# How many projection pieces stand in each of a turn's seventeen slots, in a hybrid decoder step on one NeuronCore

## The reference, cut to what matters

```python
n = rms_norm(x, g_mix)
q, k, v, xr, gr, gates = jnp.split(n @ w_in, SPLITS, axis=-1)
attn = attend(q, k, v, ...)                  # 16 heads, stick breaking
xc, rnn_buf_new = causal_dwconv(xr, rnn_buf, w_rnn_conv, b_rnn_conv)
hseq, h_last = rg_lru(xc, rnn_h0, w_rgate, b_rgate, w_igate, b_igate, rglru_lambda)
rnn = hseq * jax.nn.gelu(gr)
gate_a, gate_b = jnp.split(jax.nn.sigmoid(gates), 2, axis=-1)
x = x + (gate_a * attn + gate_b * rnn) @ w_out
...
x = x + (jax.nn.gelu(ua) * ub) @ w_down
```

## Time and profile before

| | us |
|---|---|
| median of 3 runs | 2058.79 (2057.93 to 2062.34) |
| the profiled execution | 2064.17 |
| its span on the core | 2062.5 |
| PE busy in the span | 1899.3 |
| DVE busy | 1211.0 |
| ACT busy | 929.6 |
| time per turn, scores(0) to scores(0), turns 0 to 6 | 101.4, 111.7, 109.5, 112.1, 108.5, 112.3, 108.0 |

### The profile page before, as it was taken

The page is one execution under the profiler, slowest core; times in us unless marked ns, Lnnn a source line. Parts: engine busy times, 40 slices in busy tenths (PEclk is TensorE's granted clock), DMA queues, the critical chain, the costliest instruction groups (busy, mean ns, idle before and its releaser), DMA issues. The chain is left out here.

```text
span 2062.5 us, 38464 instructions
## 1 busy us (share of the span) xinstructions
PE 1899.3 (92%) x14580; PEld 1732.3 (84%) x14580; DVE 1211.0 (59%) x1999; ACT 929.6 (45%) x1506; POOL 199.2 (10%) x98
## 2 busy tenths in 40 slices
PE   6998999989998999898996978999999999999985
PEld 5897878878787878786873768999999999999984
DVE  6101667767685858576776344755665566556655
ACT  5121677776767686768764222222222122212213
POOL 0121000000000000000000003221122112211210
PEclk9999999999999999999997988999999999999998
DMA  3334213131314232332223211211111111101104
GB/s 133 109 87 112 75 47 101 42 105 44 97 44 107 56 85 66 80 83 71 74 58 95 93 62 50 62 51 31 51 51 51 31 51 51 51 31 51 51 10 181
DMA packets 198685, 143.47 MB, mean 70 GB/s; under 512 B 58289, under 2 KB 187890, under 8 KB 198528
## 3 DMA queue, kind: packets, MB, share of 16 engines
q1 hardware_dynamic: 198554, 141.73, 23.9%
HBM read 124.31 MB, written 17.61 MB: 69 GB/s over the span
## 5 line engine op out<-in xcount | busy, mean ns | idle before, releaser
L87 PE MATMUL d_p_up<-n_hi,d_w_hi 128*128 128x346 f32 x1056 | 341.9, 324 | 14.7 <-POOL d_w_lo L1762 7.9
L87 PE MATMUL d_p_up<-n_hi,d_w_lo 128*128 128x346 f32 x1056 | 341.3, 323 | 0.0
L87 PE MATMUL d_p_up<-n_lo,d_w_hi 128*128 128x346 f32 x1056 | 341.0, 323 | 0.0
L1910 DVE TENSOR_TENSOR mix<-mix,d_p_down 128x346 f32<-128x346 f32 x264 | 136.1, 515 | 267.8 <-PE d_p_down L1959 267.8
L87 PE MATMUL b_p_proj<-n_hi,b_w_hi 128*128 128x350 f32 x768 | 264.4, 344 | 15.9 <-DVE b_w_lo L1117 9.4
L1762 POOL TENSOR_TENSOR d_w_lo<-w_raw,d_w_hi 128x1024 fp32r<-128x1024 f32 x45 | 109.1, 2426 | 1483.0 <-ACT d_w_hi L1793 1483.0
L87 PE MATMUL b_p_proj<-n_lo,b_w_hi 128*128 128x350 f32 x768 | 251.4, 327 | 0.0
L87 PE MATMUL b_p_proj<-n_hi,b_w_lo 128*128 128x350 f32 x768 | 251.3, 327 | 0.0
L1807 ACT ACTIVATE d_up<-d_p_up 128x346 f32<-128x346 f32 x132 | 60.1, 457 | 399.6 <-PE d_p_up L87 399.6
L87 PEld LDWEIGHTS d_p_up<-n_hi,d_w_hi 128*128 128x128 f32 x1056 | 200.4, 190 | 16.0 <-POOL d_w_lo L1762 8.3
L87 PEld LDWEIGHTS d_p_up<-n_lo,d_w_hi 128*128 128x128 f32 x1056 | 200.8, 190 | 0.0
(11 more groups left out here) (262 smaller groups left out, 3849.4 us busy)
## 6 DMA issues: line engine op xcount, KB each, us to landing
w_raw<-in_w_in SPq DMA_DIRECT2D x45, 512.0 KB, 4.2
w_raw<-in_w_up SPq DMA_DIRECT2D x45, 512.0 KB, 3.7
b_page<-in_cache_k SPq DMA_DIRECT2D x128, 128.0 KB, 2.1
b_page<-in_cache_v SPq DMA_DIRECT2D x128, 128.0 KB, 2.1
w_raw<-in_w_down SPq DMA_DIRECT2D x22, 512.0 KB, 3.4
b_q_in<-q_scr SPq DMA_DIRECT2D x272, 32.0 KB, 2.2
mix<-in_x_prompt SPq DMA_DIRECT2D x8, 512.0 KB, 7.9
w_raw<-in_w_out SPq DMA_DIRECT2D x8, 512.0 KB, 3.5
```

The costliest lines, as they stand in the source:

```text
L87: last = pe.matmul(out, w[:, k, :], x[:, k, col:col + width], start=(k == 0 and w is w_hi and x is x_hi), stop=(k == KT - 1 and w is w_lo))
L1910: dve.tensor_tensor(to, to, p_down[:, n % 4, 0:FW], ALU.add).then_inc(down_out, 1)
```

## The change

The number of pieces in each slot is changed. The sum stays 96, and the order of the pieces among themselves stays.

```diff
     for s in range(SLOTS):
-        count = 6 if s < 8 or s % 3 == 0 else 5
+        count = 11 if s == 0 else 6 if s < 6 else 5
         here, at = pieces[at:at + count], at + count
```

## The result

| | before | changed |
|---|---|---|
| median | 2060.57 us (4 runs) | 2114.52 us (4 runs, 2112.11 to 2115.93) |
| ratio to before | | 1.0252 (95% interval 1.0235 to 1.0268) |
| profiled span | 2062.5 us | 2114.2 us |

The change costs 52 us (1.0252 x 2060.57 - 2060.57). The forecast was 29 us, and the range ended at 2103 us. The direction and the places were right, a size was not.

The account below looks back on a forecast made before the run. PE was taken as the bound, busy 92% of the span. Turns 1 to 7 at 3.3 us each (23.2 us) plus 5.8 us in turn 0 made 29 us on 2058.8: 2088 us, range 2073 to 2103 us.

Parts of the forecast that it names:

- Part 1: Slot 0: five more pieces cost nothing in turns 1 to 7, and 2.5 us once in turn 0.
- rival E: Turn starts: cover of the fill fails, scores(0) late for ACT; up to 17.5 us more, 2105 us; 7% together with rival C.
- Part 2: Slots 6, 7, 9, 12, 15: one piece less gains 2.0 us a turn, slot 9's not gained; turn 0 gains 2.5 us.
- Parts 3 and 4: New waits: slot 10 for gr1's copy, 3.54 us a turn; slot 13 for gb0's copy, 1.28 us a turn.
- 18.1 us would have spoken against it: Sign against the forecast: slot 10's value products to slot 13's first projection staying 18.1 us, not 21 or more.
- Part 5: Clock: lower level behind slot 10's wait costs 1.5 us a turn (bounds 0 and 4.1); turn starts gain 1.0 us.
- gain by the clock at the starts: Turn starts: with the first wait filled, two spans run at full clock, gaining 1.0 us a turn (bounds 0 and 3).
- Rival B: Waits come, but the clock holds in slot 10 or turn starts win back up to 3 us; 2062 to 2076 us; 10%.
- rival D: Slot 10: ACT's copy of gr1 comes earlier, so the change gains; 2034 to 2041 us; 5%.
- Rival C: Clock drops after slot 13 too, or stays low slots 10 to 13; 2102, up to 2110 us; 7% together with rival E.

Follow-up runs that it names:

- experiment 8: Kernel before plus 15 thrown-away matmuls behind the pieces of slot 0, no piece moved; ratio to before 1.0013, 2.7 us over.
- Experiments 2: Kernel before with one piece of gr2 moved from slot 11 to slot 10 (counts 6 and 4); 2106.9 us, ratio to before 1.0205.
- experiment 3: Kernel before with one piece of gb1 moved from slot 14 to slot 13 (counts 6 and 4); ratio to before 1.0034, 7 us over.
- experiment 6: Changed kernel with two pieces of gr2 put back from slot 10 into slot 11 (counts 3 and 7); 2072.58 us, ratio to before 1.0050.
- experiment 5: Kernel before with eleven pieces in slot 0, the five extra taken from slots 3 to 7, no new bank wait; 2043.8 us, ratio to before 0.9906.
- experiment 4: Changed kernel plus 24 thrown-away matmuls in slot 10 ahead of the wait for gr1's copy; 2087.57 us, ratio to before 1.0111.
- experiment 7: Changed kernel with ACT copying gr1 in slot 10 and gb0 in slot 13 ahead of the softplus passes; 2077.63 us, ratio to before 1.0065.
- experiment 9: Changed kernel plus 12 thrown-away matmuls in slot 10's wait, in place of 24 in experiment 4; 2103.41 us, ratio to before 1.0201.
- experiment 1: Kernel before with eleven pieces in slot 0, the five extra taken from slots 1 to 5; 2056.86 us, ratio to before 0.9965.
- experiment 10: Experiment 5's version with 13 pieces in slot 0 and 4 in slots 6 and 7; 2042.46 us, ratio to before 0.9891.

## Why the prediction was wrong in its size

Summed over the eight turns of the two profiled executions, from the L1315 rows. Slot 9's piece stands in the second row, and the DVE wait that takes its gain stands in the third:

| term | forecast | measured |
|---|---|---|
| fill in turn 0 | +2.5 | +2.1 |
| five pieces out of slots 6, 7, 9, 12, 15 | -20 | -17 |
| slots 10 and 11, the wait itself | +31 | +31 |
| slots 10 and 11, the lower clock | +12 | +27 |
| slot 13 | +10 | +10 |
| starts of turns (forecast by the clock) | -7 | -6 |
| outside the stage | 0 | +4.4 |
| sum | 29 | 52 |

- **Part 1 (the fill is hidden) was right**: experiment 8, and the starts of turns, where scores(0) is not later behind scores(16) than it was (0.8 us earlier in the sum of seven). So rival E did not come either.
- **Part 2 was right** in slots 6, 7, 9 and 12 (0.45 to 0.5 us each, and slot 9 lost again in front of slot 10, where the wait for DVE grew from 0.53 to 0.99 us). Slot 15 gave only 0.2 us in turn 2.
- **Parts 3 and 4, the two new waits, were right**: 4.29 us measured where 4.47 us were worked out, and slot 13 1.26 us longer where 1.28 us were worked out. From the value products of slot 10 to the first projection of slot 13 it is 24.7 us in turn 2 (494.49 to 519.15), where 18.1 us would have spoken against it. Experiments 2, 3 and 6 show each of them alone, and experiment 5 shows that without them the change is a gain.
- **Part 5 failed**: "I take 1.5 us for each turn" for the clock behind slot 10. It is 3.64 us in turn 2 and 27 us over the kernel, by experiment 4. The bounds I gave (0 and 4.1 us) hold it; the value taken was the wrong one. I priced a spell by what slot 1 lost at the start of a turn. But there ACT and DVE hold slots 1 and 2 as well, so a slow PE costs little: in turn 3 of the changed kernel, whose start has no low clock at all, slot 1 takes 5.55 us but slot 2 then 7.58, together 13.1 us, against 13.6 to 14.5 us in turns 1 to 7 before. Behind slot 10 the others wait for PE: DVE stands idle until 506.55, and of the 4.1 us that half the clock takes from the 8.2 us of matmuls at the lower level 3.64 us were lost. With 3.6 in place of 1.5 the sum would have been 46 us. The row with 8.18 us busy in a spell was the one to price it by.
- The **gain by the clock at the starts** (1.0 us a turn) was about right in the changed kernel (6 us in seven turns); experiment 8 gives 0.6 us a turn by its trace for the same fill, and 0.4 us at most by its medians. In experiments 4, 6, 7 and 9, whose starts are those of the changed kernel, slots 15, 16, 0, 1 and 2 took 266.3 to 269.4 us over the seven starts, against 265.6 us in the changed kernel and 273.4 before, so its 6 us are at the high end of what single executions show. How much of them is the clock's stays open.
- **Rival B** (the clock holds) and **rival D** (the copy comes in time) did not come. **Rival C** gave nearly the right time (2102 to 2110 us), but not by its mechanism: the clock does not fall after slot 13 in any turn of the changed kernel or of experiment 3. It is low in slots 10 and 11, and costs more there than was charged.
- The **4.4 us outside the stage** I had not in the sum. The code there is unchanged. From the first matmul of the output projection to the end the spans are 965.0 us before, 969.5 us changed, 966.7 us in experiment 1, 968.9 us in experiment 2 and 964.0 us in experiment 3, so it moves by several us between kernels with the same code there. The clock is a part of it at most: it was at its lower level there for 75 us in the changed kernel and 67 us before, worth up to 4 us, but for 68 us in experiment 2. What sets it was not tested.

## What to carry to other kernels

Filling an engine's wait with work from a list shifts every later boundary of the list: look where each item that needs a buffer now begins against the place where that buffer is freed, since one of 96 pieces in the wrong slot cost 42 us. Price a wait on TensorE as the wait plus the slow work behind it, and look at who is on the path behind it: where the others waited for TensorE, the clock cost nearly as much (27 us) as the wait (31 us); at the starts of turns, where other engines held the path too, 20 us less of the lower clock gave back 4 us in the trace of experiment 8 and nothing in its median. And before work is taken out of a stretch in which an engine never idles, ask which chain on the other engines it covers (experiment 1).

## What the runs showed of the hardware that was not expected

Adding work made a kernel faster: 24 thrown-away matmuls in each of eight turns saved 27 us, by holding the granted clock at 1.00 where it was 0.60 for 10.2 us of busy matmuls. And the fall is not a fixed price of a wait. Behind 3.0 us (turn 0) to 4.3 us it came in each turn of the changed kernel, behind 3.3 us (experiment 2) in each of turns 1 to 7. Behind waits of 2.2 to 2.4 us the same code lost 3 us in some turns of one execution and nothing in others. It also came behind far shorter waits: in two turns of seven in experiment 6, where the longest was 1.3 us, and in three of seven in experiment 10 behind a single wait of 1.1 us, once after 36.2 us in which PE had never stopped, while the same wait in the other four turns left the clock at full. So a short wait is no assurance that the clock holds. What decides between the turns was not tested.
